# First input tile of the SSD mixer computed together with the step product, its weights prepared earlier, and a reciprocal moved from VectorE to ScalarE

## The chip, the cores and the metric

One core of a Trainium2 chip runs the whole kernel. The metric is the device time of one execution in microseconds (us), taken as the median of several runs. Engine names in rows: PE is TensorE's matmul (PEld its weight load), DVE is VectorE, ACT is ScalarE, POOL is GpSimd, SP is SyncE, which here issues most DMAs; SPq and ACTq are the queues in which an engine issues DMAs.

## The reference, cut to what matters

One decoder layer: adaLN modulation, a Mamba-2 (SSD) mixer, a residual layer norm, and a routed mixture of experts (MoE). The change touches only the beginning of the mixer:

```python
mod = silu(c) @ ada_w + ada_b                  # shift, scale, gate rows
hin = x * (1.0 + sc1) + sh1                    # 512 tokens x 1024
z, xbc, dt = split(hin @ w_in)                 # 2048, 3072 and 32 columns
xbc = silu(causal_depthwise_conv(xbc, conv_w, conv_b))
dt = softplus(dt + dt_bias)                    # 32 heads x 512 tokens
acum = cumsum(dt * a)                          # per chunk; feeds the scan
```

Softplus is written as max(v, 0) + log1p(e) with e = exp(-|v|). The log1p is made accurate by a correction: with u = 1 + e it is ln(u) + (e - (u - 1)) / u. The division by u is what the change moves from one engine to another.

## The kernel before, in words

The kernel is written out by hand for each engine. Each engine runs its own list of instructions in order, and semaphores tie the lists together. The stages are: loads and the modulation rows, the input hin, the first group's tiles, four turns of a loop over the SSD groups (the last written out apart), the router, and the MoE blocks. MoE starts some 500 us into the span.

*Modulation.* SP loads x (four pieces) and the first 2048 columns of ada_w as eight 1 MB pieces; DVE adds each piece, times one column of silu(c), to the rows accA (L997, the last piece as two halves in L1002). When the first half of the last piece is in, PE sums the rows over partitions into columns of PSUM in four steps p = 0 to 3 (L1541), eight one-column products each. The PSUM bank of a step is mod_bank(p): before the change 0, 7, 0, 7. DVE copies each step's four columns to modc (L1014). Semaphore s_rowc counts these copies.

*Input.* Eight chunks k of hin, 128 rows by 512 tokens, are made: PE transposes x (L1517; chunks 6 and 7 only inside step p = 3), DVE scales and shifts (L1019, hraw), ACT rounds to the high part (L709), and the low part, hraw less the high part, is made by POOL for even k (L567) and by DVE for odd k (L1008). High and low parts are needed since products run in fp32r: every product is made of three, high by high, high by low, low by high.

*Step product and first tiles.* After step 3 PE makes the dt product, 24 products with 32-column weights (L1578 to L1580), three for each chunk, into bank 3. It then makes the tiles i = 0 to 5 of group 0 (xbc_tile, called from a loop): each is 24 products with 128-column weights (L1553 to L1555) into bank i % 2. The weights of a tile come by one 512 KB DMA (load_x, L355) into one of two slots of stage, are rounded by ACT (unit_high, L702), and get their low part on POOL (unit_low, L561), which counts up s_ul. Tile i of 2 or more waits for s_cv, which says that the convolution of tile i - 2 has read its bank.

*Convolution.* ACT makes the first tap out of the bank (conv0, L731) and DVE adds the other three (xbc_tile on DVE, L1036, "the taps" below). ACT then applies silu (L737).

*The dt chain.* The result of the dt product goes to ACT (L715, bias), DVE makes -|v| (L1229), ACT exp (L717), DVE u, u - 1 and e less that (L1231 to L1233), ACT ln (L719), and DVE the reciprocal (L1235), the correction and max(v, 0) (L1237 to L1239), the decay and its running sums (L1243 to L1251), and their split into high and low parts (L1255 to L1263). The taps of tiles 0 to 5 stand between these steps in DVE's list. PE's list goes on after tile 5 with small products on the running sums (L1587, L1591), and then the loop over groups.

Tensors are named in rows by the region of SBUF they lie in: ssd and ssd_r hold the mixer's data, early and ssd the pieces of ada_w, both the constants and x.

## Time and profile before

| what | us |
|---|---|
| median of 3 runs | 1097.07 |
| lowest and highest run | 1096.96 and 1103.02 |
| the profiled execution | 1096.04 |
| its span, first to last instruction | 1094.3 |

The profile and all rows below are of the profiled execution, whose time lies 1.0 us under the median of the runs and 1.7 us over its own span. Starts in rows count from the span's start. A row of the timeline gives start, duration, engine, line, operation, tile written and read, shape and count, and in brackets the idle time of the engine before it with what ended it. "Granted clock" is the share of TensorE's full clock, 2.4 GHz; 0.50 is 1.2 GHz.

### The profile page before, as it was taken

How to read it: one execution, taken by the hardware profiler on the slowest of the kernel's cores; microseconds unless marked ns; L12 is line 12 of the kernel's file. 1: busy time of each engine (PE TensorE's matmuls, PEld its weight loads, DVE VectorE, ACT ScalarE, POOL GpSimd, SP SyncE). 2: the span in 40 equal slices, each digit the busy share in tenths (PEclk: the TensorE clock that was granted, in tenths of full speed). 3: DMA queues.
4: the chain of work that ended last, by engine and by line, in shares of the span. 5: the costliest groups of instructions: out<-in, count | busy, mean ns of one | idle time of the engine just before them, and what ended most of it. 6: DMA issues, size and time to landing. Idle time of an engine off the chain costs nothing.

```text
span 1094.3 us, 14999 instructions
## 1 busy us (share of the span) xinstructions
PE 1029.5 (94%) x4954; PEld 819.3 (75%) x4954; DVE 904.0 (83%) x971; ACT 613.7 (56%) x595; POOL 465.5 (43%) x295
## 2 busy tenths in 40 slices
PE   2698899999999997999999999999999999999997
PEld 1477688778877876874588888888888888888874
DVE  5897983995599367876499999998999999999987
ACT  0364463445246435450477767777777777777750
POOL 1344554555365445106133442344332442334573
PEclk9599999999999999999999999999999999999999
DMA  9337524442462345669399999999999999999971
GB/s 356 94 88 277 155 58 139 127 118 77 118 186 60 97 134 195 269 223 357 135 325 380 384 376 364 376 384 377 367 360 383 395 367 349 391 374 375 365 314 78
DMA packets 99997, 283.08 MB, mean 259 GB/s; under 512 B 9864, under 2 KB 50992, under 8 KB 82687
## 3 DMA queue, kind: packets, MB, share of 16 engines
q1 hardware_dynamic: 93322, 270.65, 68.0%
q0 software_dynamic: 5264, 11.86, 2.9%
...
q8 instruction: 16, 0.26, 0.1%
...
## 4 chain that ended last, share of the span: by engine, by line
PE 61%; DVE 4%; issue 1%; POOL 1%; ACT 1%; DMA 0%; DVEq 0%; ACTq 0%; POOLq 0%
PE ps L1858 15%; PE ps L1860 15%; PE ps L1862 15%; PE ps L1879 2%; PE ps L1553 1%; PE ps L1555 1%; PE ps L1554 1%; PE ps L1851 1%; PE ps L1842 1%; PE ps L1632 1%; DVE moe_r L1292 1%; PE ps L1652 1%; PE ps L1654 1%; PE ps L1809 1%; PE ps L1653 1%
## 5 line engine op out<-in xcount | busy, mean ns | idle before, releaser
L1292 DVE TENSOR_TENSOR moe_r<-moe,moe_r 128x2048 fp32r<-128x2048 f32 x180 | 414.5, 2321 | 56.7 <-ACT moe_r L881 56.7
L881 ACT ACTIVATE moe_r<-moe 128x2048 fp32r<-128x2048 f32 x180 | 344.8, 1928 | 124.2 <-PE ps L1862 119.2
L1858 PE MATMUL ps<-moe_r 128*128 128x512 f32 x720 | 211.0, 397 | 2.6 <-DVE moe_r L1292 2.6
L1860 PE MATMUL ps<-moe_r 128*128 128x512 f32 x720 | 205.8, 390 | 0.0
L1862 PE MATMUL ps<-moe_r 128*128 128x512 f32 x720 | 205.5, 390 | 0.0
L561 POOL TENSOR_TENSOR ssd_r<-ssd,ssd_r 128x1024 fp32r<-128x1024 f32 x56 | 137.4, 2454 | 121.6 <-ACT ssd_r L702 117.3
L1862 PEld LDWEIGHTS ps<-moe_r 128*128 128x128 f32 x720 | 135.2, 188 | 29.1
L1860 PEld LDWEIGHTS ps<-moe_r 128*128 128x128 f32 x720 | 135.1, 188 | 29.1
L1858 PEld LDWEIGHTS ps<-moe_r 128*128 128x128 f32 x720 | 131.8, 188 | 29.4 <-DVE moe_r L1292 3.9
L1553 PE MATMUL ps<-ssd_r 128*128 128x512 f32 x320 | 128.6, 402 | 1.1 <-DVE ssd L1036 1.1
...
L1555 PE MATMUL ps<-ssd_r 128*128 128x512 f32 x320 | 124.8, 390 | 0.0
L1554 PE MATMUL ps<-ssd_r 128*128 128x512 f32 x320 | 124.7, 390 | 0.0
L625 POOL TENSOR_SCALAR moe_r<-both,moe_r 128x128 fp32r<-128x128 f32 x68 | 100.2, 1486 | 3.6 <-POOL moe_r L621 3.6
L702 ACT ACTIVATE ssd_r<-ssd 128x1024 fp32r<-128x1024 f32 x54 | 56.9, 1054 | 39.3 <-PE ps L1809 39.3
L1553 PEld LDWEIGHTS ps<-ssd_r 128*128 128x128 f32 x320 | 60.1, 188 | 17.2 <-issue 3.6
L584 POOL TENSOR_TENSOR ssd<-ssd 128x384 f32<-128x384 f32 x32 | 46.6, 1458 | 61.8 <-ACT ssd L748 61.8
L1036 DVE SCALAR_TENSOR_TENSOR ssd<-ps,ssd 128x511 f32<-128x511 f32 (+2 forms) x72 | 53.5, 742 | 22.9 <-ACT ssd L731 21.1
L1554 PEld LDWEIGHTS ps<-ssd_r 128*128 128x128 f32 x320 | 60.1, 188 | 13.7 <-issue 1.7
L1555 PEld LDWEIGHTS ps<-ssd_r 128*128 128x128 f32 x320 | 60.1, 188 | 12.8
L745 ACT ACTIVATE ssd<-ssd 128x512 f32<-128x512 f32 x32 | 20.2, 631 | 82.3 <-DVE ssd L1046 82.3
L621 POOL CAST moe_r<-moe 128x20 fp32r (+1 forms) x17 | 17.1, 1007 | 95.0 <-PE ps L1832 95.0
(303 smaller groups left out, 1485.3 us busy)
## 6 DMA issues: line engine op xcount, KB each, us to landing
moe<-in_moe_w_up SPq DMA_DIRECT2D x116, 1024.0 KB, 7.2
moe<-in_moe_w_down SPq DMA_DIRECT2D x64, 1024.0 KB, 8.3
ssd<-in_ssd_w_in SPq DMA_DIRECT2D x40, 512.0 KB, 4.0
ssd<-in_ada_w SPq DMA_DIRECT2D x30, 512.0 KB, 3.9
raw<-in_moe_w_up SPq DMA_DIRECT2D x12, 1024.0 KB, 6.9
ssd<-in_ssd_w_out SPq DMA_DIRECT2D x16, 512.0 KB, 3.8
ssd<-in_ada_w SPq DMA_DIRECT2D x4, 1024.0 KB, 17.3
...
```

The lines of the kernel that those rows point to most:

```text
L561: pool.tensor_tensor(to[:, 1, :], stage[:, slot, :], to[:, 0, :].bitcast(F32), ALU.subtract).then_inc(s_ul, 1)
L625: op = pool.tensor_scalar(sel[:, t, :], iota, tabc[:, t, 4:5].bitcast(F32), None, ALU.is_equal)
L702: act.activation(wsplit[:, slot, 0, :], stage[:, slot, :], ACT.Identity).then_inc(s_uh, 1)
L881: act.activation(wr[:, part_slot(i), 0, :], ring[i % RING], ACT.Identity).then_inc(s_wh, 1)
L1036: op = dve.scalar_tensor_tensor(conv[:, i % 2, s:], ps[:, i % 2, 0:T - s], gtaps[:, k, i:i + 1], conv[:, i % 2, s:], ALU.mult, ALU.add)
L1292: dve.tensor_tensor(wr[:, part_slot(i), 1, :], ring[i % RING], wr[:, part_slot(i), 0, :].bitcast(F32), ALU.subtract).then_inc(s_wl, 1)
L1553: mm(to, wh[:, k, :], hin[:, 0, k, :], start=(k == 0), stop=False)
L1554: mm(to, wh[:, k, :], hin[:, 1, k, :], start=False, stop=False)
L1555: op = mm(to, wl[:, k, :], hin[:, 0, k, :], start=False, stop=(k == DC - 1))
L1858: mm(to[i], xh, wh[i], start=start, stop=False)
L1860: mm(to[i], xh, wl[i], start=False, stop=False)
L1862: op = mm(to[i], xl, wh[i], start=False, stop=stop)
```

## The change

Six edits that belong together. (1) SP issues the load of tile 0's weights between pieces 5 and 6 of ada_w instead of behind piece 7. (2) ACT rounds tile 0's weights before the chunks of hin instead of after chunk 4, and tile 1's after chunk 4 instead of after chunk 7. (3) POOL makes the low part of tile 0's weights before the low parts of hin instead of behind the third of them. (4) PE makes three products of tile 0 behind the three of the dt product for each chunk, so that the two finish together; since tile 0 lies in bank 0, modulation steps 1 to 3 all use bank 7, and steps 2 and 3 wait for the copy of the step just before instead of the one before that. (5) The reciprocal of u is exp(-ln u) on ACT. (6) In DVE's list each of the taps of tiles 0 to 3 moves one place back, behind more of the dt chain.

```diff
--- before.py
+++ after.py
-        mod_bank = lambda p: (0, 7)[p % 2]
+        mod_bank = lambda p: 0 if p == 0 else 7
...
@@ -335,9 +335,22 @@
             for k in range(DC):
+                if k == DC - 2:
+                    load_x(0, 0)
...
-            for i in range(NT):
+            for i in range(1, NT):
                 load_x(0, i)
...
@@ -562,11 +564,10 @@
             pool.tensor_tensor(dtsplit[1], wdt, dtsplit[0].bitcast(F32), ALU.subtract).then_inc(s_dtl, 1)
+            unit_low(0, 0)
             for k in range(0, DC, 2):
                 pool.wait_ge(s_hinh, k + 1)
                 pool.tensor_tensor(hin[:, 1, k, :], hraw[:, k % 4, :], hin[:, 0, k, :].bitcast(F32), ALU.subtract).then_inc(s_hinl, 1)
-                if k == 4:
-                    unit_low(0, 0)
             unit_low(1, 1)
             for i in range(2, XU):
...
@@ -704,12 +705,12 @@
             act.activation(aneg[0:32, :], aneg[0:32, :], ACT.Exp).then_inc(s_prea, 1)
+            unit_high(0, 0, 1)
             for k in range(DC):
                 act.wait_ge(s_hraw, k + 1)
                 act.activation(hin[:, 0, k, :], hraw[:, k % 4, :], ACT.Identity).then_inc(s_hinh, 1)
                 if k == 4:
-                    unit_high(0, 0, 1)
-            unit_high(1, 1, 1)
+                    unit_high(1, 1, 1)
...
             act.wait_ge(s_pre, 2)
             act.activation(dtv[4][0:32], dtv[2][0:32], ACT.Ln).then_inc(s_prea, 1)
+            act.wait_ge(s_pre, 3)
+            act.wait_ge(s_prea, 4)
+            act.activation(dtv[2][0:32], dtv[4][0:32], ACT.Exp, scale=-1.0).then_inc(s_prea, 1)
...
             unit_high(4, 0, 3)
-            act.wait_ge(s_pre, 10)
+            act.wait_ge(s_pre, 9)
             act.activation(dtv[1][0:32], dtv[1][0:32], ACT.Exp).then_inc(s_prea, 1)
...
@@ -1231,13 +1235,11 @@
             step(dve.tensor_scalar(uv, ev, 1.0, None, ALU.add))
             step(dve.tensor_scalar(cv, uv, -1.0, None, ALU.add))
             step(dve.tensor_tensor(cv, ev, cv, ALU.subtract))
-            dve.wait_ge(s_prea, 4)
-            step(dve.reciprocal(uv, uv))
-            xbc_tile(0, 0)
+            dve.wait_ge(s_prea, 5)
             step(dve.tensor_tensor(cv, cv, uv, ALU.mult))
             step(dve.tensor_tensor(cv, cv, lv, ALU.add))
             step(dve.scalar_tensor_tensor(v, v, 0.0, cv, ALU.max, ALU.add))
-            xbc_tile(0, 1)
+            xbc_tile(0, 0)
...
             step(dve.tensor_tensor(ev.rearrange("p (c t) -> p c t", t=P), acum3[:, :, P - 1:P].broadcast_to([32, TT, P]), acum3, ALU.subtract))
-            xbc_tile(0, 2)
+            xbc_tile(0, 1)
...
             dve.wait_ge(s_dtv, 5 + G)
             dve.tensor_copy(every8r, every8).then_inc(s_dtv, 1)
+            xbc_tile(0, 2)
+            dve.wait_ge(s_prea, 6)
+            step(dve.tensor_tensor(stk[64:96], ev, v, ALU.mult))
             xbc_tile(0, 3)
-            dve.wait_ge(s_prea, 5)
-            step(dve.tensor_tensor(stk[64:96], ev, v, ALU.mult))
             xbc_tile(0, 4)
...
@@ -1530,7 +1533,7 @@
                 elif p >= 2:
                     pe.wait_ge(s_adaA, DC + 1)
-                    pe.wait_ge(s_rowc, 4 + p - 1)
+                    pe.wait_ge(s_rowc, 4 + p)
...
@@ -1573,20 +1576,27 @@
             pe.wait_ge(s_dtl, 1)
             pe.wait_ge(s_hraw, 3)
+            pe.wait_ge(s_ul, 1)
+            wh, wl = parts(0, DC, P)
             for k in range(DC):
                 pe.wait_ge(s_hinv if k % 2 else s_hinl, k // 2 + 1)
...
                 op = mm(ps[0:32, 3, :], dtsplit[1][:, k, :], hin[:, 0, k, :], start=False, stop=(k == DC - 1))
-            op.then_inc(s_dtp, 1)
-            for i in range(NT):
+                if k == DC - 1:
+                    op.then_inc(s_dtp, 1)
+                mm(bank(0), wh[:, k, :], hin[:, 0, k, :], start=(k == 0), stop=False)
+                mm(bank(0), wh[:, k, :], hin[:, 1, k, :], start=False, stop=False)
+                op = mm(bank(0), wl[:, k, :], hin[:, 0, k, :], start=False, stop=(k == DC - 1))
+            op.then_inc(s_unit, 1)
+            for i in range(1, NT):
                 xbc_tile(0, i)
             pe.wait_ge(s_dtv, 6 + G)
             acl = acg.rearrange("p g (c t) -> p (g c) t", t=P)
...
             op.then_inc(s_tokp, 1)
-            pe.wait_ge(s_pre, 11)
+            pe.wait_ge(s_pre, 10)
```

ACT's list in the place of the dt chain, before; the first three rows are the rounding of tile 0's weights between chunks 0 to 4 and 5 to 7 of hin:

```order
L709 ACTIVATE ssd_r<-ssd 128x512 [waits s_hraw] x5
L702 ACTIVATE ssd_r<-ssd 128x1024 [waits ld_u0]
L709 ACTIVATE ssd_r<-ssd 128x512 [waits s_hraw] x3
L702 ACTIVATE ssd_r<-ssd 128x1024 [waits ld_u1]
L715 ACTIVATE ssd<-ps,both 32x512 [waits s_dtp]
L717 ACTIVATE ssd<-ssd 32x512 [waits s_pre]
L719 ACT_TABLE_LOAD
L719 ACTIVATE ssd<-ssd 32x512 [waits s_pre]
L731 ACTIVATE ssd<-ps,ssd 128x512 [waits s_gtap,s_unit]
```

And the same place of ACT's list now (L703 is the rounding of weights, L711 that of hin, L716 to L723 the dt chain, L735 the first tap):

```order
L703 ACTIVATE ssd_r<-ssd 128x1024 [waits ld_u0]
L711 ACTIVATE ssd_r<-ssd 128x512 [waits s_hraw] x5
L703 ACTIVATE ssd_r<-ssd 128x1024 [waits ld_u1]
L711 ACTIVATE ssd_r<-ssd 128x512 [waits s_hraw] x3
L716 ACTIVATE ssd<-ps,both 32x512 [waits s_dtp]
L718 ACTIVATE ssd<-ssd 32x512 [waits s_pre]
L720 ACT_TABLE_LOAD
L720 ACTIVATE ssd<-ssd 32x512 [waits s_pre]
L723 ACT_TABLE_LOAD [waits s_prea]
L723 ACTIVATE ssd<-ssd 32x512 [waits s_pre]
L735 ACTIVATE ssd<-ps,ssd 128x512 [waits s_gtap,s_unit]
```

The weights moved ahead of the chunks, and a table load and a second exponential stand between the logarithm and the first tap of tile 0.

POOL's list before, from the low part of the dt weights (L564) on; L567 is the low part of a chunk of hin, L561 that of a tile's weights:

```order
L564 TENSOR_TENSOR ssd_r<-ssd,ssd_r 128x256 [waits s_dth]
L567 TENSOR_TENSOR ssd_r<-ssd,ssd_r 128x512 [waits s_hinh] x3
L561 TENSOR_TENSOR ssd_r<-ssd,ssd_r 128x1024 [waits s_uh]
L567 TENSOR_TENSOR ssd_r<-ssd,ssd_r 128x512 [waits s_hinh]
L561 TENSOR_TENSOR ssd_r<-ssd,ssd_r 128x1024 [waits s_uh] x5
```

And now, with L566, L570 and L563 in their place:

```order
L566 TENSOR_TENSOR ssd_r<-ssd,ssd_r 128x256 [waits s_dth]
L563 TENSOR_TENSOR ssd_r<-ssd,ssd_r 128x1024 [waits s_uh]
L570 TENSOR_TENSOR ssd_r<-ssd,ssd_r 128x512 [waits s_hinh] x4
L563 TENSOR_TENSOR ssd_r<-ssd,ssd_r 128x1024 [waits s_uh] x5
L575 MEMSET both 128x4096 [waits s_xtp]
```

The low part of tile 0's weights now follows the dt weights directly, with no chunk of hin ahead of it.

DVE's list from the correction (L1233, e less u - 1) to the taps of tile 1, before; L1036 are the taps, L1235 the reciprocal:

```order
L1233 TENSOR_TENSOR ssd<-ssd 32x512 [waits s_pre]
L1235 RECIPROCAL ssd<-ssd 32x512 [waits s_prea,s_pre]
L1036 SCALAR_TENSOR_TENSOR ssd<-ps,ssd 128x511 [waits s_cv0,s_pre]
L1036 SCALAR_TENSOR_TENSOR ssd<-ps,ssd 128x510 [waits s_tap]
L1036 SCALAR_TENSOR_TENSOR ssd<-ps,ssd 128x509 [waits s_tap]
L1237 TENSOR_TENSOR ssd<-ssd 32x512
L1238 TENSOR_TENSOR ssd<-ssd 32x512 [waits s_pre]
L1239 SCALAR_TENSOR_TENSOR ssd<-ssd 32x512 [waits s_pre]
L1036 SCALAR_TENSOR_TENSOR ssd<-ps,ssd 128x511 [waits s_cv0,s_pre]
```

And now (L1040 are the taps, L1239 to L1241 the three steps behind the division, L1245 to L1253 the decay and its sums):

```order
L1237 TENSOR_TENSOR ssd<-ssd 32x512 [waits s_pre]
L1239 TENSOR_TENSOR ssd<-ssd 32x512 [waits s_prea,s_pre]
L1240 TENSOR_TENSOR ssd<-ssd 32x512 [waits s_pre]
L1241 SCALAR_TENSOR_TENSOR ssd<-ssd 32x512 [waits s_pre]
L1040 SCALAR_TENSOR_TENSOR ssd<-ps,ssd 128x511 [waits s_cv0,s_pre]
L1040 SCALAR_TENSOR_TENSOR ssd<-ps,ssd 128x510 [waits s_tap]
L1040 SCALAR_TENSOR_TENSOR ssd<-ps,ssd 128x509 [waits s_tap]
L1245 TENSOR_SCALAR ssd<-ssd,both 32x512 [waits s_dtv]
L1247 COPY ssd<-ssd 32x512 [waits s_dtv]
L1249 SCALAR_TENSOR_TENSOR ssd<-both,ssd 32x128 x4
L1253 TENSOR_TENSOR ssd<-ssd 32x512 [waits s_pre]
L1040 SCALAR_TENSOR_TENSOR ssd<-ps,ssd 128x511 [waits s_cv0,s_pre]
```

The reciprocal is gone, and the taps of tile 0 stand behind the three steps that wait for ACT's second exponential (s_prea).

## Rows read from the trace of the kernel before

**Rows 1.** The page: TensorE's busy time over the whole span

```profile
PE 1029.5 (94%) x4954; PEld 819.3 (75%) x4954; DVE 904.0 (83%) x971; ACT 613.7 (56%) x595; POOL 465.5 (43%) x295
```

**Rows 2.** Who PE waited for: waiter <- engine, line; total us, times, longest

```profile
PE ps L1600 <- ACT ssd L748: 6.4, 8, 1.0
PE ps L1775 <- DVE ssd L1063: 5.0, 3, 1.7
...
PE ps L1609 <- ACT ssd L759: 1.7, 1, 1.7
```

**Rows 3.** Timeline, all engines, modulation rows and columns, from 32.95 us

```profile
32.95 1.18 POOL L564 TENSOR_TENSOR ssd_r<-ssd,ssd_r 128x256 fp32r<-128x256 f32 x1 [29.11 <-ACT ssd_r L704]
33.65 2.63 DVE L997 SCALAR_TENSOR_TENSOR ssd<-ssd,both 128x2048 f32<-128x2048 f32 x1
34.18 0.20 ACT L706 ACTIVATE both<-both 32x1 f32<-32x1 f32 x1
36.32 2.48 DVE L1002 SCALAR_TENSOR_TENSOR ssd<-early,both,ssd 128x1024 f32<-128x1024 f32 x2
...
37.75 5.25 PE L1541 MATMUL ps<-both,ssd 128*128 128x1 f32 x24 [14.91 <-DVE ssd L1002]
...
42.86 1.95 PE L1517 MATMUL ps<-both 128*128 128x128 f32 x8
...
43.66 0.14 DVE L1014 COPY both<-ps 128x4 f32<-128x4 f32 x1
```

**Rows 4.** Issues of piece 6 and tile 0's weights; their size and us to landing

```profile
8.01 0.69 SPq L342 DMA_DIRECT2D ssd<-in_ada_w  x1
...
11.77 5.61 SPq L355 DMA_DIRECT2D ssd<-in_ssd_w_in  x1
...
ssd<-in_ada_w SPq DMA_DIRECT2D x1, 1024.0 KB, 23.5
...
ssd<-in_ssd_w_in SPq DMA_DIRECT2D x1, 512.0 KB, 24.1
```

**Rows 5.** Timeline: start of the dt product, start of the reading of its result

```profile
46.17 0.61 PE L1578 MATMUL ps<-ssd_r 128*32 128x512 f32 x1
...
53.39 0.68 ACT L715 ACTIVATE ssd<-ps,both 32x512 f32<-32x512 f32 x1 [1.69 <-PE ps L1580]
```

**Rows 6.** Timeline: the dt chain on ACT and DVE, from 55.59 us

```profile
55.59 1.28 ACT L719 ACT_TABLE_LOAD   x1
...
56.89 0.63 ACT L719 ACTIVATE ssd<-ssd 32x512 f32<-32x512 f32 x1
...
57.72 3.34 DVE L1235 RECIPROCAL ssd<-ssd 32x512 f32<-32x512 f32 x1
...
61.09 2.32 DVE L1036 SCALAR_TENSOR_TENSOR ssd<-ps,ssd 128x511 f32<-128x511 f32 x3
...
64.03 0.68 DVE L1238 TENSOR_TENSOR ssd<-ssd 32x512 f32<-32x512 f32 x1
```

**Rows 7.** Timeline: a low part on POOL and one on DVE beside it

```profile
46.44 2.37 POOL L561 TENSOR_TENSOR ssd_r<-ssd,ssd_r 128x1024 fp32r<-128x1024 f32 x1
...
47.27 2.09 DVE L1008 TENSOR_TENSOR ssd_r<-ssd,ssd_r 128x512 fp32r<-128x512 f32 x1
```

**Rows 8.** Two stretches of DVE's list: bounds, length, busy us and (xcount) per engine, clock

```profile
67.69:71.36 3.67, 3.67 (x18) 3.02 (x17) 3.56 (x8) 2.42 (x4) 0.82 (x1) 1.00 0.45 118
73.60:79.31 5.71, 5.71 (x27) 4.72 (x26) 5.61 (x9) 3.64 (x4) 2.67 (x2) 1.00 0.34 92
```

**Rows 9.** Granted clock (PEclk) behind PE's wait of 4.9 us at 423 us

```profile
428.00:430.00 2.00, 1.74 (x17) 1.77 (x19) 1.98 (x4) 0.88 (x2) 0.19 (x1) 0.58 0.94 303
430.00:432.00 2.00, 2.00 (x25) 2.00 (x23) 0.45 (x1) 0.64 (x2) 1.27 (x1) 0.57 1.02 387
```

**Rows 10.** Timeline of PE: tile 5 and the first product behind it

```profile
81.67 0.50 PE L1553 MATMUL ps<-ssd_r 128*128 128x512 f32 x1 [1.10 <-DVE ssd L1036]
...
87.24 0.95 PE L1587 MATMUL ps<-ssd_r 128*128 128x16 f32 x8
```

14 lines of the change are left out of this document (7 added, 7 removed).

## The prediction

> **What bounds the kernel now.** I read the page first: PE is busy 94% of the span [rows 1], so a change matters where it makes PE start later, wait, or stop waiting. The list of PE's waits comes second. After the start PE waits little: 6.4 us in eight waits for ACT, 5.0 us in three for DVE, 1.7 us in one [rows 2]. The timeline of the first 90 us comes third, since all six edits lie there. Three things are to be seen. PE starts the modulation products at 37.75, when DVE has added the last piece of ada_w [rows 3]. From the dt product at 46.17 [rows 5] to the first small product behind tile 5 at 87.24, PE waits once, 1.10 us before tile 5, for the taps of tile 3 [rows 10]. A tile takes about 5.5 us (81.67 to 87.24 less the slow first product). Beside it DVE works without a pause on the dt chain and the taps: 3.56 of 3.67 us and 5.61 of 5.71 us are busy [rows 8]. So PE leads here by 1.1 us at most, and DVE's list is the next bound. Behind 87.24 all engines go on from where PE is, so I measure the change by what it does to the start of that product.
>
> **The shared turn of POOL and DVE.** At 46.44 POOL makes a low part, 2.37 us. DVE starts one of its own at 47.27 and takes 2.09 us, though 512 elements of this kind take about 0.7 us [rows 6, 7]. It ended 0.55 us after POOL. The same in the other order: POOL's piece at 32.95 began while DVE added a piece of ada_w, took 1.18 us, and the DVE piece behind it took 2.63 us, where the two halves of the last piece together take 2.48 [rows 3]. I read this as one turn for both engines, an instruction at a time, where the one that waits goes next. The taps read PSUM and only one tile; I take it that they need no turn, since three of them took 2.32 us in the middle of POOL's work for tile 2 [rows 6].
>
> **Part by part.**
>
> *Load of tile 0 ahead of piece 6.* Piece 6 lands at 8.01 + 23.5 = 31.5, tile 0's weights at 11.77 + 24.1 = 35.9 [rows 4]. Between them lie 1.5 MB in 4.4 us, so 0.5 MB is 1.5 us. Piece 6 then lands at 33.0, and DVE takes it at 33.65. Piece 7 lands at 35.9 at the latest and is taken at 36.32 and, its second half, near 37.5 [rows 3]. Cost nothing, with 0.6 us of cover; without the cover it would be up to 0.9 us. Tile 0's weights are in by 33.0.
>
> *High and low part of tile 0's weights early.* ACT is free at 34.4 [rows 3] and takes some 1.0 us (an estimate: 512 elements take 0.63 with the fixed part [rows 6], here are 1024), so POOL asks for its turn at 35.4, in the middle of DVE's piece 6. By the turn rule it gets it at 36.3 and holds it 2.4 us, and DVE's last piece, ready at 36.32, waits. That piece is what PE waits for at 37.75. Cost between 0 and 2.4; I take 2.2, since a waiting DVE instruction ended 0.55 rather than 0.7 us after POOL [rows 7]. What is removed, the same work at 46.44, delayed only a chunk that PE takes much later.
>
> *Bank 7 for steps 1 to 3.* PE's transposes of chunks 6 and 7 stood at 42.86 and did not wait. Now they wait for the copy at 43.66, which DVE makes behind other work, and start at 43.9 [rows 3]. Behind them in PE's list stand step 3 and the dt product. Cost 1.0 (bounds 0.8 and 1.1). The dt product starts at 46.17 + 2.2 + 1.0 = 49.4.
>
> *Chunk by chunk.* PE did not wait inside the dt product, so nothing is gained: 48 products take as long as before, and tile 0 ends 3.2 us late. But the dt result comes 5.5 us less three products later. Before, ACT read it 7.2 us after the start [rows 5]. Now 21 more products of 0.23 us lie before it: 49.4 + 7.2 + 4.8 = 61.4. Tile 0 ends at 61.9, tile 1 at 67.4.
>
> *The chain.* From ACT's reading to the end of the correction's subtraction, 53.39 to 57.72, is 4.3 us, and the logarithm ends 4.1 us after 53.39. So the logarithm is done at 65.5. The new exponential needs a table load in front of it, and the order shows that this load waits for the logarithm: 1.30 + 0.63 gives 67.5 [rows 6]. Before, the reciprocal took 3.34 us in this place, so 1.4 us of it is truly saved. Three steps of 0.68 follow, then the taps of tile 0, 2.3 us: 71.9. POOL's low part of tile 2, which starts when ACT has made the first tap, ends at about 72.0.
>
> *The taps one place back.* Before, they stood behind the reciprocal and were done at 63.4, ahead of PE. Now tile 2 starts at 72.0, and PE has waited 4.6 us. DVE's stretch to the taps of tile 1 was 3.67 us, 0.7 of it a wait for POOL's turn [rows 8]. Now the low part of tile 3 falls into it in full, 2.3 us, so the taps of tile 1 end at 71.9 + 5.3 + 2.3 = 79.5. Tile 2 ended at 77.5: a wait of 2.0. The stretch to the next taps was 5.71 us with one full wait for POOL in it and has one again, for tile 4's weights (5.9 taken): 87.7. Tile 3 ended at 85.0: a wait of 2.7. Tile 4 runs to 93.2, tile 5 to 98.7, with the taps of tile 3 done by 91, so the old wait of 1.10 is gone.
>
> *Sum.* 2.2 + 1.0 + 4.6 + 2.0 + 2.7 - 1.1 = 11.4, or 98.7 against 87.24. The profiled execution of 1096.04 becomes 1107.4. It lies 1.0 under the median, so I say 1108.5 for the median. Without any of the three waits for POOL's turn the same walk gives 1.0 + 4.6 - 1.1 = 4.5 or 4.6, because PE then has less to wait for after tile 2: 1101.6.
>
> **The clock.** After PE's wait of 4.9 us at 423 the granted clock fell to 0.58 and 0.57 for two stretches of 2 us [rows 9], that is to 1.2 GHz for most of them, 1.7 us lost. I expect it behind the first wait too. There it costs nothing: tile 2 ends at 79.2 and its successor waits until 79.5 anyway. Behind the wait of 2.7 it would cost in full.
>
> **A rule weighed.** The rows have the logarithm starting 0.02 us behind the table load, 1.30 for the whole switch [rows 6]. The Trainium skill, "ScalarE: Activation LUTs", section "What ACT_TABLE_LOAD costs", says that a switch costs 1.28 us of load and 1.38 us of drain. By that the chain would be 1.4 us longer and the median an estimated 1109.9. The same page, section "Table sets: the hidden batching unit", says that ln followed by exp needs one load because one set holds both. By that the new load would not be there and the median an estimated 1107.2; but the order of the changed kernel shows the load.
>
> **The rivals.**
>
> *A, the forecast:* all three waits for POOL's turn. 1108.5, give or take 1.5. For it: each rests on an instruction of the same kind that did wait. Against it: they need the times to meet within 2 us. Chance 0.41.
>
> *B, the turns meet only in part.* One or two of three: 4.6 to 9, about 1104. For it: of four such places before, one cost only 0.7. Chance 0.26.
>
> *C, the clock falls again,* behind the wait before tile 4, and tile 4 runs 1.7 us longer: 1110.2. For it: rows 9. Against it: that wait was longer, 4.9 against 2.7, and the 1.10 before tile 5 brought no fall. Chance 0.20.
>
> *D, the switch of tables is dearer than its row,* since here the load itself waits for a result: up to 1.4 more, 1109.9. Chance 0.06.
>
> *E, not slower.* ACT and DVE reach the loop over groups early in relation to PE and give back what PE waited for them there: a fourth of 6.4, one of the three waits of 5.0, and the 1.7, together 5.0 us [rows 2]. With B's lower end of 4.6 the median is 1096.7. It decides only if the loss is under 5 us and those waits are bound to time and not to PE's own products. Against it: they stand behind work that PE's tiles release. Chance 0.05.
>
> That the change brings what it is written for, less waiting for chunks, would need such waits; there are none to remove. Faster by over 1% has 0.02.
>
> **How the numbers follow.** One per cent, about what a measurement of this kernel can tell from no change, is 11 us, up to 1108.0. A lies across it (0.45 of it below), B and E below, C and D above. Same: 0.18 + 0.26 + 0.05 = 0.49, of which I give 0.01 to faster. Slower: 0.23 + 0.20 + 0.06 = 0.49, rounded to 0.50. The range goes from B's low end, 1101.5, to A with C and half of D, 1111.5; E and both C and D in full are left out.
>
> **What would show it.** In the profile after: DVE's last piece of ada_w ends near 40.9 instead of 38.8, with a duration over 3 us for the first half; the transposes of chunks 6 and 7 wait about a microsecond; ACT reads the dt result near 61.4; a table load in front of the second exponential; PE waits of about 4.6, 2.0 and 2.7 us before tiles 2, 3 and 4 and none before tile 5; the first small product at 98.7. The prediction is wrong if the modulation products start at 37.8 as before, if tile 2 starts before 70, or if the loop over groups takes back more than 2 us.

## The result and the profile after

The changed kernel takes 1107.51 us (median of 8 runs, 1105.50 to 1109.18), the kernel before 1096.91 (8 runs, 1095.36 to 1103.02). The ratio is 1.0084, with a 95% interval of 1.0063 to 1.0105. It is not the quotient of the two medians (1.0097); two of the eight runs before lie near 1103, which a median doesn't show. The prediction was 1108.5, in 1101.5 to 1111.5, with 0.50 on slower by over 1% and 0.48 on within 1%; the time lies inside the range, and the ratio just inside 1%, on the side that had 0.48. The profiled execution took 1108.90, its span is 1107.1 (before: 1094.3), its mean granted clock 0.978 (before: 0.984).

The page's first part of the changed kernel. Columns as in [rows 1]:

```profile
PE 1034.3 (93%) x4954; PEld 821.2 (74%) x4954; DVE 904.9 (82%) x970; ACT 615.5 (56%) x597; POOL 467.3 (42%) x295
```

PE has as many matmuls as in [rows 1] and is busy 4.8 us longer; some of that is the clock (below), the rest of the 12.8 us is waiting.

The list of PE's waits of the changed kernel (waiter, releaser, total us, times, longest), to be held against [rows 2]:

```profile
PE ps L1610 <- ACT ssd L752: 6.4, 8, 1.0
PE ps L1556 <- DVE ssd L1040: 5.7, 2, 4.7
...
PE ps L1785 <- DVE ssd L1067: 4.3, 3, 1.5
...
PE ps L1619 <- ACT ssd L763: 1.6, 1, 1.6
```

The second row has two waits for the taps (line 1040), 4.7 and 1.1 us; before there was one of 1.10 [rows 10]. The other three are those of [rows 2]: 6.4, 4.3 instead of 5.0, and 1.6 instead of 1.7. The loop gave back 0.8 us, not 5.

The timeline of the changed kernel, modulation rows and columns. [Rows 3] are the same stretch before:

```profile
30.95 2.62 DVE L1001 SCALAR_TENSOR_TENSOR ssd<-early,both,ssd 128x2048 f32<-128x2048 f32 x1
...
32.20 3.58 POOL L563 TENSOR_TENSOR ssd_r<-ssd,ssd_r 128x1024 fp32r<-128x1024 f32 x1 [0.77 <-ACT ssd_r L703]
33.67 4.25 DVE L1001 SCALAR_TENSOR_TENSOR ssd<-ssd,both 128x2048 f32<-128x2048 f32 x1
37.96 2.48 DVE L1006 SCALAR_TENSOR_TENSOR ssd<-early,both,ssd 128x1024 f32<-128x1024 f32 x2
39.39 3.54 PE L1544 MATMUL ps<-both,ssd 128*128 128x1 f32 x16 [17.57 <-DVE ssd L1006]
...
45.30 0.14 DVE L1018 COPY both<-ps 128x4 f32<-128x4 f32 x1
...
45.55 1.94 PE L1520 MATMUL ps<-both 128*128 128x128 f32 x8 [0.43 <-issue]
...
48.85 0.61 PE L1583 MATMUL ps<-ssd_r 128*32 128x512 f32 x1
```

POOL and DVE take turns here: POOL's low part of tile 0 meets DVE's piece 6, which takes 4.25 us, and 2.35 when nothing holds it up (a_no_meet below). The products start 1.64 later than in [rows 3]. The transposes of chunks 6 and 7 start 6.16 us behind the products' start, not 5.11, since they stand behind the copy at 45.30. The step product starts at 48.85, 2.68 later than in [rows 5].

The dt chain and the first taps of the changed kernel, all engines, from 61.99 us; [rows 5, 6 and 8] are the same work before:

```profile
61.99 0.68 ACT L716 ACTIVATE ssd<-ps,both 32x512 f32<-32x512 f32 x1 [9.97 <-PE ps L1585]
...
65.50 0.63 ACT L720 ACTIVATE ssd<-ssd 32x512 f32<-32x512 f32 x1
...
66.21 1.28 ACT L723 ACT_TABLE_LOAD   x1
67.50 0.63 ACT L723 ACTIVATE ssd<-ssd 32x512 f32<-32x512 f32 x1
...
68.24 0.68 DVE L1239 TENSOR_TENSOR ssd<-ssd 32x512 f32<-32x512 f32 x1 [1.94 <-ACT ssd L723]
...
69.82 5.07 POOL L563 TENSOR_TENSOR ssd_r<-ssd,ssd_r 128x1024 fp32r<-128x1024 f32 x2 [15.62 <-ACT ssd_r L703]
...
70.38 2.32 DVE L1040 SCALAR_TENSOR_TENSOR ssd<-ps,ssd 128x511 f32<-128x511 f32 x3
...
72.61 2.56 DVE L1245 TENSOR_SCALAR ssd<-ssd,both 32x512 f32<-32x512 f32 x1
...
72.75 0.79 PE L1556 MATMUL ps<-ssd_r 128*128 128x512 f32 x1 [4.65 <-DVE ssd L1040]
...
77.74 2.32 DVE L1040 SCALAR_TENSOR_TENSOR ssd<-ps,ssd 128x511 f32<-128x511 f32 x3
...
83.13 2.19 DVE L1265 CAST ssd_r<-both 128x8 fp32r<-128x8 f32 x1
...
87.60 0.50 PE L1556 MATMUL ps<-ssd_r 128*128 128x512 f32 x1 [1.10 <-DVE ssd L1040]
...
98.62 0.95 PE L1597 MATMUL ps<-ssd_r 128*128 128x16 f32 x8
```

PE waits 4.65 us before tile 2 because the taps of tile 0 end at 72.7, and 1.10 before tile 4. There is no wait before tile 3, where 2.0 had been foreseen, and none before tile 5. The first small product starts at 98.62, 11.38 later than in [rows 10].

Why no wait before tile 3 is in the windows of the changed kernel (columns as in [rows 8], the granted clock stands third from the end):

```profile
70.00:72.00 2.00, 0.00 (x0) 0.00 (x0) 1.89 (x4) 1.98 (x3) 2.00 (x1) 0.88 0.00 0
72.00:74.00 2.00, 1.25 (x3) 1.06 (x4) 2.00 (x2) 1.28 (x2) 2.00 (x2) 0.50 0.08 16
74.00:76.00 2.00, 2.00 (x6) 1.52 (x6) 1.95 (x4) 0.00 (x0) 0.89 (x1) 0.50 0.89 248
76.00:78.00 2.00, 2.00 (x6) 1.55 (x5) 1.93 (x6) 0.00 (x0) 0.00 (x0) 0.50 0.92 253
78.00:80.00 2.00, 2.00 (x10) 1.65 (x9) 1.93 (x4) 0.00 (x0) 0.00 (x0) 0.92 0.03 7
```

The clock is at 0.50 (1.2 GHz) from 72 to 78. Tile 2 takes 8.1 us (72.75 to 80.88) instead of 5.5, and the taps of tile 1 are done at 80.06, before it ends.

### The profile page after: what moved, and what is told of

The parts are those of the page before. It is cut to its first block, busy times and chain, and to the rows that moved or that the text cites. A ratio compares the mean times of both kernels' runs of the same rounds, so it can differ in the third digit from the quotient of the medians.

```text
span 1107.1 us, 15001 instructions
## 1 busy us (share of the span) xinstructions
PE 1034.3 (93%) x4954; PEld 821.2 (74%) x4954; DVE 904.9 (82%) x970; ACT 615.5 (56%) x597; POOL 467.3 (42%) x295
## 4 chain that ended last, share of the span: by engine, by line
PE 60%; DVE 4%; issue 2%; POOL 1%; ACT 1%; DMA 0%; DVEq 0%; ACTq 0%; POOLq 0%
PE ps L1868 15%; PE ps L1870 14%; PE ps L1872 14%; PE ps L1889 2%; PE ps L1556 1%; PE ps L1557 1%; PE ps L1558 1%; PE ps L1861 1%; PE ps L1852 1%; PE ps L1642 1%; DVE moe_r L1295 1%; PE ps L1662 1%; PE ps L1664 1%; PE ps L1663 1%; PE ps L1818 1%
## 5 line engine op out<-in xcount | busy, mean ns | idle before, releaser
L1868 PE MATMUL ps<-moe_r 128*128 128x512 f32 x720 | 211.1, 397 | 3.4 <-DVE moe_r L1295 3.4
L563 POOL TENSOR_TENSOR ssd_r<-ssd,ssd_r 128x1024 fp32r<-128x1024 f32 x56 | 138.8, 2479 | 131.6 <-ACT ssd_r L703 126.9
L1868 PEld LDWEIGHTS ps<-moe_r 128*128 128x128 f32 x720 | 131.7, 188 | 30.5 <-DVE moe_r L1295 5.1
L1556 PE MATMUL ps<-ssd_r 128*128 128x512 f32 x312 | 126.8, 406 | 5.7 <-DVE ssd L1040 5.7
L1558 PE MATMUL ps<-ssd_r 128*128 128x512 f32 x312 | 122.6, 393 | 0.0
L1557 PE MATMUL ps<-ssd_r 128*128 128x512 f32 x312 | 122.5, 393 | 0.0
L703 ACT ACTIVATE ssd_r<-ssd 128x1024 fp32r<-128x1024 f32 x54 | 56.9, 1053 | 39.5 <-PE ps L1819 39.5
L1556 PEld LDWEIGHTS ps<-ssd_r 128*128 128x128 f32 x312 | 59.2, 190 | 21.9 <-DVE ssd L1040 6.6
L1040 DVE SCALAR_TENSOR_TENSOR ssd<-ps,ssd 128x511 f32<-128x511 f32 (+2 forms) x72 | 53.5, 743 | 26.3 <-ACT ssd L735 24.5
L1557 PEld LDWEIGHTS ps<-ssd_r 128*128 128x128 f32 x312 | 59.3, 190 | 13.5 <-issue 1.7
L1558 PEld LDWEIGHTS ps<-ssd_r 128*128 128x128 f32 x312 | 59.1, 190 | 12.7
```

The source lines that it names most:

```text
L563: pool.tensor_tensor(to[:, 1, :], stage[:, slot, :], to[:, 0, :].bitcast(F32), ALU.subtract).then_inc(s_ul, 1)
L703: act.activation(wsplit[:, slot, 0, :], stage[:, slot, :], ACT.Identity).then_inc(s_uh, 1)
L1040: op = dve.scalar_tensor_tensor(conv[:, i % 2, s:], ps[:, i % 2, 0:T - s], gtaps[:, k, i:i + 1], conv[:, i % 2, s:], ALU.mult, ALU.add)
L1556: mm(to, wh[:, k, :], hin[:, 0, k, :], start=(k == 0), stop=False)
L1557: mm(to, wh[:, k, :], hin[:, 1, k, :], start=False, stop=False)
L1558: op = mm(to, wl[:, k, :], hin[:, 0, k, :], start=False, stop=(k == DC - 1))
```

## The experiments

Twelve kernels ran. A number for each comes first, because the executions are shifted among themselves: the modulation products start anywhere from 35.0 to 40.0, also in kernels that don't touch what stands ahead of them. "Between" is the time from the start of the products to the first small product. It is the sum of the next two columns, parted where ACT reads the result of the step product. "Rest" is span less first small product. Read from the profiles' timelines:

| kernel | products start | first small product | between | to the reading | behind the reading | rest | median us (runs) | ratio to before, interval |
|---|---|---|---|---|---|---|---|---|
| before | 37.75 | 87.24 | 49.49 | 15.64 | 33.85 | 1007.1 | 1096.91 (8) | 1 |
| changed | 39.39 | 98.62 | 59.23 | 22.60 | 36.63 | 1008.5 | 1107.51 (8) | 1.0084, 1.0063-1.0105 |
| a_unmixed | 39.28 | 93.26 | 53.98 | 17.65 | 36.33 | 1008.7 | 1103.83 (7) | 1.0058, 1.0034-1.0081 |
| a_no_meet | 38.65 | 97.16 | 58.51 | 22.10 | 36.41 | 1008.1 | 1104.26 (5) | 1.0058, 1.0037-1.0079 |
| a_banks | 38.99 | 96.47 | 57.48 | 21.06 | 36.42 | 1008.4 | 1106.81 (5) | 1.0085, 1.0057-1.0112 |
| a_recip | 39.63 | 100.88 | 61.25 | 22.44 | 38.81 | 1009.0 | 1110.63 (4) | 1.0113, 1.0087-1.0139 |
| a_busy | 36.90 | 94.65 | 57.75 | 21.26 | 36.49 | 1008.9 | 1106.46 (4) | 1.0100, 1.0060-1.0140 |
| a_taps | 40.04 | 96.69 | 56.65 | 21.96 | 34.69 | 1009.3 | 1110.36 (6) | 1.0078, 1.0063-1.0093 |
| b_early | 39.28 | 94.33 | 55.05 | 16.78 | 38.27 | 1008.9 | 1098.38 (10) | 1.0005, 0.9985-1.0025 |
| b_exp | 37.09 | 90.07 | 52.98 | 16.67 | 36.31 | 1009.6 | 1101.21 (12) | 1.0034, 1.0015-1.0052 |
| b_exp_warm | 35.03 | 86.30 | 51.27 | 14.96 | 36.31 | 1008.8 | 1100.34 (12) | 1.0030, 1.0011-1.0049 |
| b_taps_back | 36.60 | 91.31 | 54.71 | 16.02 | 38.69 | 1011.5 | 1102.39 (11) | 1.0012, 0.9993-1.0032 |
| b_exp_taps | 36.58 | 91.52 | 54.94 | 16.62 | 38.32 | 1008.0 | 1100.84 (12) | 0.9989, 0.9971-1.0006 |
| b_exp_taps_warm | 37.89 | 90.92 | 53.03 | 14.96 | 38.07 | 1008.0 | 1102.21 (11) | 1.0007, 0.9993-1.0021 |

Names with a_ are the changed kernel with one thing undone or added, those with b_ the kernel before with one part of the change. The kernel before itself had a median of 1096.93 beside a_unmixed, a_no_meet, a_banks and a_recip (12 runs), 1096.50 beside a_busy, b_early, b_exp and b_exp_warm (29 runs), and 1102.09 beside b_taps_back, b_exp_taps, b_exp_taps_warm and a_taps (29 runs). These three groups ran on three chips, so across them ratios and not medians are compared. Why the kernel before can differ by 6 us is found under b_exp_taps. Its 1096.93 beside the first four is that of the result, so the medians of those four can be held against 1107.51. But the interval of every a_ kernel overlaps that of the changed kernel: what a part costs is read from the profiles, and the times can only agree with it.

Part of "between" is no edit's doing. Nothing ahead of the reading differs in the kernels before, b_taps_back, b_exp_taps and b_exp, yet they take 15.64, 16.02, 16.62 and 16.67 to it. All of that spread lies in the step product (7.22 to 8.25 us from its start to the reading): the clock comes up behind 8 of its 24 products in the first and behind 13 in the last, and each costs 0.43 instead of 0.23 us until then. In the changed kernel and its variants with mixed products the same stretch takes 11.81 (a_busy) to 13.14 us (changed). A difference of up to 1.3 us ahead of the reading is therefore not put down to an edit. Behind the reading the numbers are steadier: 36.41 to 36.63 in three kernels that are alike there (changed, a_no_meet, a_banks), 36.31 in b_exp and in b_exp_warm.

**a_unmixed: edit 4 undone.** The step product first, then tile 0, the rest as changed:

```
                 if k == DC - 1:
                     op.then_inc(s_dtp, 1)
+            for k in range(DC):
                 mm(bank(0), wh[:, k, :], hin[:, 0, k, :], start=(k == 0), stop=False)
```

> The changed kernel with one thing undone: the dt product is finished first and tile 0 made behind it. Theory (the late dt result starts every later wait): ACT reads the dt result about 5 us earlier, near 57 instead of 61.99, the wait of 4.65 us before tile 2 shrinks to about 1, and since DVE's list sets the start of tile 4, the first small product behind tile 5 comes near 94 instead of 98.62: median 1103, 4 to 5 us below the 1107.5 of the changed kernel. Rival (the loss comes from the early weights and the bank waits, ahead of the dt product): no more than 1 us gained, median 1107.

ScalarE reads the step product at 56.93 instead of 61.99, the taps of tile 0 start at 65.32 instead of 70.38, PE has no long wait before tile 2, and the clock stays up. To the reading it is 4.95 less, behind it 0.30 less. PE's remaining waits:

```profile
75.00 0.50 PE L1556 MATMUL ps<-ssd_r 128*128 128x512 f32 x1 [1.57 <-DVE ssd L1040]
...
82.24 0.50 PE L1556 MATMUL ps<-ssd_r 128*128 128x512 f32 x1 [1.50 <-DVE ssd L1040]
```

So doing tile 0 chunk by chunk is the largest part of the loss: it makes the step product 5 us late, and the chain behind it is what PE waits for. Two waits for taps stay, before tiles 3 and 4; a_taps, b_exp and b_taps_back are about them.

**a_no_meet: POOL's low part of tile 0 kept away from DVE's row pieces.**

```
+            pool.wait_ge(s_adaA, DC + 1)
             unit_low(0, 0)
```

> The changed kernel, but POOL starts the low part of tile 0's weights only after DVE has added the last piece of ada_w. Theory (POOL and DVE have one turn, and DVE's piece 6 waited): that piece takes 2.35 us instead of 4.25, the last one ends at 38.8 or a little less instead of 40.4, the first small product behind tile 5 comes 1.6 us earlier, at 97.0, median 1105.9. Rival (the piece was late because its load landed late behind tile 0's weights): the piece still ends near 37.9, nothing gained, median 1107.5.

The row pieces in this kernel:

```profile
34.83 2.35 DVE L1002 SCALAR_TENSOR_TENSOR ssd<-ssd,both 128x2048 f32<-128x2048 f32 x1
37.21 2.48 DVE L1007 SCALAR_TENSOR_TENSOR ssd<-early,both,ssd 128x1024 f32<-128x1024 f32 x2
38.65 2.69 PE L1545 MATMUL ps<-both,ssd 128*128 128x1 f32 x12 [15.45 <-DVE ssd L1007]
...
39.77 2.35 POOL L563 TENSOR_TENSOR ssd_r<-ssd,ssd_r 128x1024 fp32r<-128x1024 f32 x1 [7.20 <-DVE ssd L1007]
```

The same piece takes 2.35 instead of 4.25, POOL's own part 2.35 instead of 3.58. From the start of piece 5 to the end of the last piece it is 7.60 us, in the changed kernel 9.49: the turn costs 1.9. The wait before tile 2 stays (4.67). The first small product is 1.46 earlier. To the reading it is 0.50 less, no more than the spread there. The median is 3.3 us lower than that of the changed kernel, more than the turn can give; five runs with times from 1103.6 to 1107.0 don't settle the rest.

**a_banks: banks of the modulation steps as before.**

```
-        mod_bank = lambda p: 0 if p == 0 else 7
+        mod_bank = lambda p: (0, 7)[p % 2]
-                    pe.wait_ge(s_rowc, 4 + p)
+                    pe.wait_ge(s_rowc, 4 + p - 1)
```

and a wait for the last copy ahead of the mixed products, since bank 0 is theirs.

> The changed kernel with the modulation steps in banks 0, 7, 0, 7 and their old waits, and one wait for the third copy ahead of the dt product. Theory: the transposes of chunks 6 and 7 no longer wait for that copy, everything behind them comes 1.0 us earlier, median 1106.5. Rival (the transposes are hidden, since PE would wait for DVE's chunks anyway): nothing, 1107.5.

The products run in one group of 24 without a break, and the transposes of chunks 6 and 7 start 5.11 behind their start again, 1.05 less, as foreseen. Between is 1.75 less, but 0.50 of that is the step product's clock. The median doesn't show it: 0.7 us lower than that of the changed kernel, with an interval 6 us wide.

**a_recip: edit 5 undone.** The exponential on ScalarE taken out, `step(dve.reciprocal(uv, uv))` back ahead of the correction:

> The changed kernel with the reciprocal back on DVE, all else as changed. Theory: the reciprocal of 3.34 us would end at 69.7 where the second exponential let DVE go on at 68.24, so everything that hangs on DVE's list comes 1.4 us later: first small product near 100.0, median 1108.9. Rival (PE's own half clock in tile 2 sets what follows): nothing, 1107.5.

The foreseen gain of 1.4 for edit 5 was too small. DVE's list in this kernel:

```profile
66.41 3.34 DVE L1236 RECIPROCAL ssd<-ssd 32x512 f32<-32x512 f32 x1
67.89 5.09 POOL L563 TENSOR_TENSOR ssd_r<-ssd,ssd_r 128x1024 fp32r<-128x1024 f32 x2 [13.44 <-ACT ssd_r L703]
69.78 1.00 DVE L1237 TENSOR_TENSOR ssd<-ssd 32x512 f32<-32x512 f32 x1
70.82 2.71 DVE L1238 TENSOR_TENSOR ssd<-ssd 32x512 f32<-32x512 f32 x1
...
74.28 2.32 DVE L1037 SCALAR_TENSOR_TENSOR ssd<-ps,ssd 128x511 f32<-128x511 f32 x3
```

Besides the 3.34 us, the multiplication and the addition behind it wait for POOL (1.00 and 2.71 instead of 0.68 each, 2.35 more). The taps of tile 0 start 3.9 later than in the changed kernel, and PE waits 8.47 before tile 2. Later waits go in exchange: behind the reading it is 2.2 more, and the median is 3.1 higher (1109.86 to 1111.62, against 1105.50 to 1109.18). In the changed kernel the exponential is the one part that helps, and it helps by more than its own time, since it gets DVE past the place before POOL comes.

**a_busy: PE kept busy in its wait before tile 2.** Nineteen products that nothing reads:

```
             for i in range(1, NT):
+                if i == 2:
+                    for j in range(19):
+                        mm(ps[0:32, 7, :], dtsplit[0][:, 0, :], hin[:, 0, 0, :], start=True, stop=True)
```

> The changed kernel with 19 products of no use (weights of the dt product, chunk 0, into bank 7) in PE's list before tile 2, so that PE is busy in its wait; the result is the same. Theory (DVE's list sets the start of tile 4, and the half clock in tile 2 is hidden in front of it): the granted clock stays at 1.00 and tile 2 takes 5.5 us instead of 8.1, but tile 4 starts at 87.6 and the small product at 98.6 as before: median 1107.5. Rival (the half clock is part of the loss): 2.7 us gained, small product at 95.9, median 1104.8.

```profile
68.92 0.49 PE L1556 MATMUL ps<-ssd_r 128*128 128x512 f32 x1 [0.26 <-DVE ssd L1040]
...
76.36 0.50 PE L1556 MATMUL ps<-ssd_r 128*128 128x512 f32 x1 [1.71 <-DVE ssd L1040]
...
83.60 0.50 PE L1556 MATMUL ps<-ssd_r 128*128 128x512 f32 x1 [1.50 <-DVE ssd L1040]
```

The granted clock is 1.00 in all windows from 64 to 78. Now the foreseen wait before tile 3 is there, 1.71, and the one before tile 4 is 1.50. Between is 57.75, 1.5 less, but 1.34 of it lies ahead of the reading, where nothing was changed. Behind the reading it is 36.49 against 36.63: of the 2.6 us that the low clock took in tile 2, all but 0.1 would have been waiting. The theory held, DVE's list sets the start of tile 4 (25.6 us behind the reading in the changed kernel, 25.4 here). The four times (1105.24 to 1112.41) don't add to it.

**b_early: edits 1 to 3 alone in the kernel before** (load ahead, low part early, second weight tile early):

```
             for k in range(DC):
+                if k == DC - 2:
+                    load_x(0, 0)
...
+            unit_low(0, 0)
             for k in range(0, DC, 2):
```

> The kernel before with only edits 1 to 3: tile 0's weights loaded, rounded and split early. Theory (the low part on POOL holds up DVE's piece 6): piece 6 takes over 4 us, the modulation products start 1.6 us later than 37.75, first small product at 88.9, median 1098.5. Rival (the early weights cost nothing alone): 1096.9.

DVE's piece 6 takes 4.25 here too and the products start at 39.28, 1.53 later than in [rows 3]. Behind the reading it is 38.27 against 33.85, which these edits don't explain. The median is 1.9 us above that of the kernel before, not separable. The profiled execution took 1104.92, 6.5 over its own median; the likely reason of both follows under b_exp_taps.

**b_exp: edits 5 and 6 alone in the kernel before.**

```
+            act.activation(dtv[2][0:32], dtv[4][0:32], ACT.Exp, scale=-1.0).then_inc(s_prea, 1)
-            step(dve.reciprocal(uv, uv))
-            xbc_tile(0, 0)
...
             step(dve.scalar_tensor_tensor(v, v, 0.0, cv, ALU.max, ALU.add))
-            xbc_tile(0, 1)
+            xbc_tile(0, 0)
```

> The kernel before with only edits 5 and 6: the reciprocal as an exponential on ACT and the taps of tiles 0 to 3 one place back, dt product first, weights and banks as before. Theory: here the chain has 5 us more cover, tile 2 starts at 64.1 as before, DVE's list is about 2 us shorter, the wait of 1.10 before tile 5 goes, first small product at 86.1 instead of 87.24, median 1095.8 against 1096.9. Rival (the longer chain on ACT, a table load and an exponential, is itself what loses): tile 2 waits, the small product comes later than 87.24, median 1098 or more.

Missed: slower, 1.0034. PE's waits in it:

```profile
71.80 0.50 PE L1555 MATMUL ps<-ssd_r 128*128 128x512 f32 x1 [1.58 <-DVE ssd L1039]
79.05 0.50 PE L1555 MATMUL ps<-ssd_r 128*128 128x512 f32 x1 [1.51 <-DVE ssd L1039]
```

Tile 2 doesn't wait, since the chain is early enough; but the taps of tile 1 start at 69.43 behind a subtraction that waited for POOL (2.70 for 0.68), where in the kernel before they stood ahead of it. Between is 3.5 more, 2.5 of it behind the reading and 1.0 in the step product's clock.

**b_exp_warm:** b_exp with 56 products that nothing reads in PE's wait for the rows of ada_w, so that the clock is up for the modulation products.

> The kernel before with edits 5 and 6 and 56 products of no use (zeros, into bank 7) in PE's wait for the rows of ada_w, up to about 37 us; the result is the same. Theory (PE runs at half clock from 37.75 to 49.4 because it idled): modulation products, transposes and the first dt products run at full clock, DVE's chunks become the bound of the dt product, the small product behind tile 5 comes 2 to 3 us earlier than in the kernel with edits 5 and 6 alone, median 1093.5. Rival (the products of one column do not depend on the clock, or the clock falls again in between): no gain, 1095.8.

The 24 products take 3.54 us instead of 5.25 and the first small product comes 1.7 nearer to them; behind the reading nothing changes (36.31 in both). No more than that is won, because the granted clock fell again: the products follow a wait of 1.94 us, and it is 0.74 from 36 to 38 us and 0.50 from 38 to 46, though PE has products in all that time, and the step product takes 8.25 us to the reading as in b_exp. Of the 1.7 less than 1 us is seen in the median (1100.34 to 1101.21, intervals of 4 us).

**b_taps_back: edit 6 alone in the kernel before.** The taps of tiles 0 to 3 one place later, the reciprocal where it was.

> The kernel before with edit 6 alone: the reciprocal stays on VectorE, each tile's taps stand one place later. If the place of the taps is the cause: taps of tile 0 start near 63.2, PE waits about 1.5 before tile 3 and 1.5 before tile 4, the first small product comes 52.5 to 54.5 us behind the start of the modulation products (before: 49.49), and the median is 1100 to 1102. If the place is harmless: 49.5 and 1097.

Between is 54.71, 5.2 more, 4.8 of it behind the reading. PE waits 3.17 before tile 2 and 1.11 before tile 4, not 1.5 before 3 and 4: the reciprocal and a wait for POOL (2.50 for 0.68 behind it) push the taps of tile 0 to 64.28, and the clock falls behind the first wait as in the changed kernel. Yet the ratio is 1.0012 only. A reason is argued under the next kernel.

**b_exp_taps: edit 5 alone.** As b_exp, but the taps in their old places:

```
             step(dve.tensor_tensor(cv, ev, cv, ALU.subtract))
+            xbc_tile(0, 0)
             dve.wait_ge(s_prea, 5)
             step(dve.tensor_tensor(cv, cv, uv, ALU.mult))
```

> The kernel before with edit 5 alone: the exponential on ScalarE, and the taps of tiles 0 to 3 on VectorE in their old places (those of tile 0 ahead of the wait for the exponential). If it is edit 6 that cost 4 us in the run of edits 5 and 6 together: taps of tile 0 start near 61 as before, PE waits neither before tile 3 nor before tile 4, the first small product starts 49.5 us behind the modulation products' start as before (49.49) or up to 1 earlier, and the median is 1095.5 to 1097. If the exponential on ScalarE costs it (1.9 us more on ScalarE's list, ahead of the taps and of the high parts it makes): 52 to 53 us behind the start and about 1100.

PE waits neither before tile 3 nor before tile 4, as foreseen. But between is 54.94, neither 49.5 nor 52 to 53, and behind the reading it is 38.32, 4.5 more than before. DVE and POOL in this profile:

```profile
76.79 2.40 POOL L561 TENSOR_TENSOR ssd_r<-ssd,ssd_r 128x1024 fp32r<-128x1024 f32 x1 [3.03 <-ACT ssd_r L702]
76.80 5.88 DVE L1265 CAST ssd_r<-both 128x8 fp32r<-128x8 f32 x1
...
79.14 3.52 POOL L574 MEMSET both<- 128x4096 f32 x1
...
84.32 0.66 PE L1555 MATMUL ps<-ssd_r 128*128 128x512 f32 x1 [3.94 <-DVE ssd L1039]
```

and in the profile of the kernel before, in the same place:

```profile
71.53 2.40 POOL L561 TENSOR_TENSOR ssd_r<-ssd,ssd_r 128x1024 fp32r<-128x1024 f32 x1 [3.02 <-ACT ssd_r L702]
73.60 0.61 DVE L1255 CAST ssd_r<-ssd 32x512 fp32r<-32x512 f32 x1
...
76.97 2.40 POOL L561 TENSOR_TENSOR ssd_r<-ssd,ssd_r 128x1024 fp32r<-128x1024 f32 x1 [3.04 <-ACT ssd_r L702]
...
76.98 2.42 DVE L1263 CAST ssd_r<-both 128x8 fp32r<-128x8 f32 x1
79.31 3.55 POOL L574 MEMSET both<- 128x4096 f32 x1
```

A cast of eight elements, 0.17 us when nothing is in its way (at 84.95 in a_recip), asks for the turn 0.01 us behind POOL's low part. Before, it went next, and the memset of 4096 elements ran behind. Here the memset went next, and the cast took 5.88: all of the low part and all of the memset. PE then waits 3.94 before tile 5. A multiplication of two tiles isn't held up by the memset: the one in L1266 takes 0.68 us at 81.65 in the kernel before, in the middle of it. The Trainium skill, "SBUF — State Buffer", section "Who interferes with whom", says that a cast can enter a mode that takes the port pair shared with GpSimd, and that whoever holds the pair keeps it for the whole instruction. By that rule the traces agree: the cast is blocked for 2.4 us in one and for 2.4 and 3.5 in the other, while three taps with one input from SBUF took 2.3 us beside POOL [rows 6].

That the two ask within 0.01 us of each other is no accident. The cast of L1255 above (0.61 us, and 0.41 at 79.97 in the changed kernel, where POOL is idle) ends 0.28 behind POOL's low part of tile 4's weights, so it seems to have waited for it; 2.77 later DVE asks for the small cast. POOL's next low part comes 5.44 behind the last, one tile of PE, and 2.40 + 0.28 + 2.77 is 5.45. The same sum, within 0.02, stands in the profiles of b_early, b_exp_taps, b_exp_taps_warm and a_taps. In a_taps the cast was 0.01 us ahead of POOL instead of behind it:

```profile
87.81 0.17 DVE L1266 CAST ssd_r<-both 128x8 fp32r<-128x8 f32 x1
87.82 2.42 POOL L563 TENSOR_TENSOR ssd_r<-ssd,ssd_r 128x1024 fp32r<-128x1024 f32 x1 [3.04 <-ACT ssd_r L703]
```

The same 5.88 or 5.89 us stands in the profiles of b_early and b_exp_taps_warm. Behind the reading these three kernels take 38.07 to 38.32, and the kernel before 33.85: a lost turn costs 4.2 to 4.5 us there, the fall of the clock behind the longer wait included. With their longer rest, 0.9 to 1.8, it is 5.1 to 6.2 us.

The single times of the kernel before fit that: its 29 beside b_exp are 22 from 1093.6 to 1097.5 and 7 from 1098.9 to 1103.3; on the chip of b_exp_taps 6 of 29 lie below 1098.3, 21 above 1100.9 and 2 between. I read the two groups as the turn won and the turn lost; that is argued, not shown. Three profiles of a lost one in variants and one of a won one in the kernel itself speak for it; a profile of the kernel before with a lost turn isn't there; b_early, which differs from it only ahead of the first products, is the nearest. Against it stands b_exp_warm: its cast is 7 us ahead of the memset, and its times spread over 7.8 us all the same (1096.88 to 1104.68), so the turn isn't all that moves a time.

Edit 6 ends the meeting: with the taps of one tile fewer ahead of it, the cast starts 7.1 us before the memset in b_exp. Behind the reading edit 6 alone (b_taps_back, 38.69) takes 4.8 us more than the won turn and 0.4 more than the lost one of b_early; with edit 5 (b_exp, 36.31) it takes 2.0 less than the lost turn of b_exp_taps. That this is why its ratio is 1.0034 on one chip and 1.0012 on the other is argued: neither b_exp nor b_taps_back ran on both.

**a_taps: edit 6 undone in the changed kernel.** The same places of the taps, in the changed kernel.

> The changed kernel without edit 6: the taps of tiles 0 to 3 in their old places. If the place of the taps is the cause of a part of the loss here too: taps of tile 0 start near 68.8 instead of 70.4, PE's wait before tile 2 is 3.1 instead of 4.65, the first small product starts 56 to 57.7 us behind the modulation products' start (changed kernel: 59.23), and the median is 1103.5 to 1106. If the late result of the dt product alone sets it, because VectorE has the same work to do in either order: 59 and 1107.5.

Between is 56.65, 2.6 less than in the changed kernel and inside what was expected if the places matter; 1.9 of it lies behind the reading. But PE's wait before tile 2 is 4.24 and not 3.1: the taps of tile 0 start at 68.92, and then POOL's low part of tile 2 comes last.

```profile
69.83 5.12 POOL L563 TENSOR_TENSOR ssd_r<-ssd,ssd_r 128x1024 fp32r<-128x1024 f32 x2 [14.97 <-ACT ssd_r L703]
...
72.32 0.77 PE L1556 MATMUL ps<-ssd_r 128*128 128x512 f32 x1 [4.24 <-POOL ssd_r L563]
```

The time doesn't tell: a ratio of 1.0078, with 1.0084 for the changed kernel, and six times from 1107.7 to 1112.2. The meeting of cast and memset is back in this kernel. Its profiled execution, the fastest of the six, is one where the cast came first, and it isn't shown how the others went.

**b_exp_taps_warm:** b_exp_taps with the 56 products of b_exp_warm.

> The kernel before with edit 5 alone and 56 products without a use while PE waits for the rows of ada_w, so that its clock is up when the modulation products start. The first small product comes 1.7 us nearer to the modulation products' start than without them (b_exp_taps), as it was with the taps one place back. If that gain passes through the loop: a median 1.0 to 1.7 lower than that run, 1094 to 1095.5. If VectorE's list takes its place as the bound: within 0.5 of that run. Between them it shows whether a version with edit 5 is faster than the kernel before (1096.5) at all.

Between is 1.9 less than in b_exp_taps (both with the turn lost), 1.66 of it ahead of the reading; the ratio is 1.0007, no better than 0.9989, so the gain isn't seen in the time. No version ran that is faster than the kernel before beyond its interval; the nearest is b_exp_taps, 0.9989 (0.9971 to 1.0006). Moving the memset away from the cast, the direct test of the lost turn, wasn't tried.

## Why the prediction was right

The mechanism was the forecast's: a late step product, PE waiting for taps, POOL's turns between. Its sum of 11.4 for the first small product measured 11.38, but not all of its terms did, and that they add up so closely is luck: the result of the step product was read 0.6 later than foreseen, and from there to the first small product it took 36.6 and not 37.3.

- *Load ahead of piece 6, nothing.* Right. DVE's pieces follow each other as in [rows 3].
- *POOL's turn, 2.2.* It measured 1.64 at the start of the products, 1.9 against a_no_meet. The place was another: POOL asked at 32.20 and not at 35.4, since the small weights for dt had landed earlier, and so it was piece 6 that waited and not the last.
- *Bank 7, 1.0.* It measured 2.68 - 1.64 = 1.04.
- *Chunk by chunk, result of the step product at 61.4.* It was read at 61.99. The product began 0.55 earlier than foreseen, but 13 of its products ran at the low clock (0.43 us each), where 8 did before. The sum had no term for these: 13.14 us from start to reading are 1.1 more than the 12.0 of the forecast.
- *The wait of 4.6 before tile 2.* Measured 4.65; tile 1's end was 0.7 and the end of the taps 0.8 later than foreseen. Rival D fell: the load took 1.28, and the exponential started 0.01 behind it. The Trainium skill, "ScalarE: Activation LUTs", section "What ACT_TABLE_LOAD costs", adds 1.38 of drain to a switch; this trace doesn't show it. Nor does it show the single set for ln and exp of the section "Table sets: the hidden batching unit": a load stands between them.
- *The wait of 2.0 before tile 3.* This step failed. POOL's turn did fall there (72.61, 2.56 us) and the taps of tile 1 were done at 80.06 (foreseen 79.5), but tile 2 ended at 80.88 and not at 79.2. I had sized the low clock by the two stretches of [rows 9] (1.7 us); here it was low for three, and tile 2 took 2.6 us longer. That the low clock there "costs nothing" held all the same: a_busy, with the clock held, has the wait back (1.71) and is only 0.1 us shorter behind the reading. The clock took the place of waits.
- *The wait of 2.7 before tile 4.* Measured 1.10, because tile 3 ended later by what the clock had cost. Tile 4 started at 87.60 (foreseen 87.7), since DVE's list and not PE's sets that start. That it came so close has luck in it: tile 2 started 0.75 later than foreseen, and DVE's two stretches to the ends of the next taps took 7.4 and 7.5 us, where the sum had 7.6 and 8.2.
- *No wait before tile 5; clock not falling behind tile 4's wait (rival C).* Right, no wait and 5.5 us per tile.
- *Rival B* fell since all three turns met nearly in full (1.64 to 1.9, 2.1 and 2.0 us); *rival E* fell by the table's column of rests: 1008.0 to 1011.5 in all thirteen others, 1007.1 in the kernel before. Of its waits one group gave back 0.7, and a later one in the MoE blocks, L1858 before and L1868 now, grew from 2.6 to 3.4. What is lost ahead of the first small product is lost, whatever the edits; and the base of the sum was the lowest rest of all, so the profiled execution was 1108.9 and not 1107.4. The forecast then put the median 1.0 above the profiled execution, as before; it came 1.4 below. The two errors, +1.5 and -2.4, leave the 1.0 by which 1108.5 missed 1107.51. The profile of the base was one with the turn of cast and memset won, which the forecast didn't know of.

The prediction did not price edits 5 and 6 apart. It took 1.4 for edit 5 (measured 2.2 behind the reading, 3.1 in the median) and told edit 6 only as part of the waits. Undone one by one, and measured where each acts, the mixing gives back 4.95, the bank 1.05 and edit 6 1.9 (in an execution where the cast came ahead of POOL), and edit 5 takes 2.2. They need not add up to the 9.7 by which between grew, since they act on the same waits and the clock differs by up to 1.3. In the kernel before edit 5 alone wins nothing that shows: behind the reading 38.32 (b_exp_taps) against 38.27 (b_early), both with a lost turn.
